# Sixteen pairs of gate tiles of a two-block model, each computed as seven half-width products instead of two full-width tiles

## The reference, cut to what matters

```python
h = rmsnorm_2(x, pre_norm_g[l])
proj = h @ w_in[l]
(u, v, z_a, c_q, c_kv, k_rope, z_b, x_c, z_c,
 g_a, g_b, g_c) = jnp.split(proj, cuts, axis=-1)
y_a = gmlp_spatial(u, v, ...) * jax.nn.silu(z_a)
y_b = mla_attention(c_q, c_kv, k_rope, ...) * jax.nn.silu(z_b)
y_c = rg_lru(x_c, ...) * jax.nn.silu(z_c)
merged = (jax.nn.sigmoid(g_a) * (y_a @ w_proj_a[l])
          + jax.nn.sigmoid(g_b) * (y_b @ w_proj_b[l])
          + jax.nn.sigmoid(g_c) * (y_c @ w_proj_c[l]))
x = x + rmsnorm_2(merged @ w_out[l], post_norm_g[l])
```

## Time and profile before

| | |
|---|---|
| median of 3 runs | 3152.47 us (3151.99 to 3153.68) |
| profiled execution, first to last instruction (span) | 3150.8 us |
| its PE busy time | 3140.4 us, 100% of the span |
| DVE, ACT, POOL busy | 59%, 40%, 13% |
| granted TensorE clock, mean | 1.000 |
| DMA | 110 GB/s on average |

### The profile page before, as it was taken

One profiled execution on the slowest core, in us unless ns is written; L12 is line 12 of the kernel. 1 busy time (PEld: TensorE's weight loads), 2 busy tenths in 40 slices (PEclk: granted clock), 3 DMA queues, 4 the chain that ended last, 5 costly groups with the idle time before them and its releaser, 6 DMA issues.

```text
span 3150.8 us, 36896 instructions
## 1 busy us (share of the span) xinstructions
PE 3140.4 (100%) x14840; PEld 2628.4 (83%) x14840; DVE 1859.9 (59%) x2504; ACT 1258.6 (40%) x1889; POOL 394.9 (13%) x287
## 2 busy tenths in 40 slices
PE   9999999999999999999999999999999999999999
PEld 8888888888888888888888888888888888888887
DVE  6876456665687655665557642447656754344754
ACT  4323334434433334443445422226635442223742
POOL 1201112110020121112012000110011100011001
PEclk9999999999999999999999999999999999999999
DMA  4332323235442223222642232223332222323432
GB/s 170 116 101 94 101 94 108 100 123 191 149 121 96 97 89 113 96 98 97 204 144 88 78 102 92 89 94 118 124 132 73 82 94 96 98 87 96 138 99 102
DMA packets 105354, 345.42 MB, mean 110 GB/s; under 512 B 13824, under 2 KB 14080, under 8 KB 104416
## 3 DMA queue, kind: packets, MB, share of 16 engines
q1 hardware_dynamic: 101856, 328.47, 32.1%
q0 software_dynamic: 3184, 14.06, 1.3%
q10 hardware_dynamic: 144, 0.52, 0.1%
HBM read 324.65 MB, written 2.10 MB: 104 GB/s over the span
## 4 chain that ended last, share of the span: by engine, by line
PE 96%; DVE 3%; ACT 1%; DMA 0%; SPq 0%; issue 0%; POOL 0%; POOLq 0%
PE ps L520 94%; DVE r L1484 1%; PE ps L611 1%; DVE wl L1474 1%; PE ps L852 0%; DVE f L1489 0%; SPq L2261 0%; DVE f L1552 0%; DMA X<-x_in 0%; DMA f<-f 0%; DVE r L1900 0%; DVE f L1722 0%; ACT wh L982 0%; ACT f L1308 0%; DVE sm L1921 0%; PE ps L564 0%
## 5 line engine op out<-in xcount | busy, mean ns | idle before, releaser
L520 PE MATMUL ps<-h,wh 128*128 128x512 f32 (+1 forms) x5824 | 1695.3, 375 | 0.7 <-DVE wl L1474 0.3
L520 PEld LDWEIGHTS ps<-h,wh 128*128 128x128 f32 x5824 | 1063.4, 188 | 200.1 <-issue 3.4
L520 PE MATMUL ps<-h,wl 128*128 128x512 f32 (+1 forms) x2912 | 1091.2, 375 | 0.0
L1474 DVE TENSOR_TENSOR wl<-raw,wh 128x1024 fp32r<-128x1024 f32 (+1 forms) x583 | 739.1, 1280 | 294.9 <-ACT wh L982 293.7
L982 ACT CAST wh<-raw 128x1024 fp32r<-128x1024 f32 (+2 forms) x596 | 592.3, 1006 | 685.9 <-PE ps L520 684.7
L520 PEld LDWEIGHTS ps<-h,wl 128*128 128x128 f32 x2912 | 547.1, 188 | 98.9
L520 PE MATMUL ps<-r,wh 128*128 128x512 f32 x1536 | 473.4, 389 | 0.9 <-DVE r L1484 0.5
L520 PEld LDWEIGHTS ps<-r,wh 128*128 128x128 f32 x1536 | 288.1, 188 | 62.2 <-issue 2.1
L1074 ACT CAST r<-f 128x512 fp32r<-128x512 f32 x194 | 119.8, 621 | 517.1 <-DVE f L1820 149.0
L520 PE MATMUL ps<-r,wl 128*128 128x512 f32 x792 | 304.3, 389 | 0.0
L520 PE MATMUL ps<-wh,r 128*128 128x512 f32 x960 | 302.4, 390 | 0.3
(11 more groups left out here) (160 smaller groups left out, 2133.5 us busy)
## 6 DMA issues: line engine op xcount, KB each, us to landing
raw<-wst SPq DMA_DIRECT2D x544, 512.0 KB, 3.3
raw<-wst SPq DMA_DIRECT2D x48, 320.0 KB, 3.0
r<-r SPq DMA_DIRECT2D x64, 128.0 KB, 2.3
f<-gains POOLq DMA_DIRECT2D x6, 1024.0 KB, 5.2
raw<-wst SPq DMA_DIRECT2D x20, 256.0 KB, 3.0
f<-f SPq DMA_DIRECT2D x72, 64.0 KB, 2.0
f<-tab POOLq DMA_DIRECT2D x16, 256.0 KB, 4.4
X<-x_in SPq DMA_DIRECT2D x4, 512.0 KB, 8.2
```

What stands on the lines that cost most here:

```text
L520: return e.matmul(o, a, b, start=start, stop=stop, skip_group_check=True)
L1474: e.tensor_tensor(l[:, 0:WIDTH[c]], raw[:, c % NRAW, 0:WIDTH[c]], h[:, 0:WIDTH[c]].bitcast(F32), ALU.subtract).then_inc(*lo_cut.up(("lo", c)))
```

## The change

In each of the two layers of the second block eight pairs of neighbouring gate tiles, gateb (3,4), (5,6), gatea and gatec (2,3), (4,5), (6,7), are computed together. A pair is a product of a 2x2 arrangement (first and second four tiles of k, first and second gate tile of the weights) with a 2x2 arrangement of h (first and second four tiles of k, first and second half of the rows). It is written in seven products of blocks in place of eight (Strassen's scheme in Winograd's form), each of 4 x 3 = 12 matmuls of 256 columns: p1, n5, p2, u2, p3, u3, c21. Around them:

- *Weights.* Four sums of weight blocks of a pair (128x512 each) are made by POOL (`sums`). The seven blocks (three raw, four sums) are cut in pieces of 512 columns, as chunks *0 to *3.
- *h.* Four combinations of h's blocks (`mixed`, 128x1024 each) are made once per layer by POOL (`mix`: ten steps of two pieces of 128x2x256) behind the first head's scores; ACT casts and DVE takes the low part of one of them at each of the heads 3 to 6. They lie where X was: X is saved to DRAM at the layer's start (`save_rows`) and loaded back at its end (`rows_back`).
- *Combining.* ACT copies p1, n5, u2 and u3 out of PSUM (`kept`, line 1329, 128x256). DVE makes c11, c12, c22 (lines 1984 to 1993). The sigmoids take 128x256, 128x512 and 128x256 elements. TensorE waits for the copy of p1 before u2, of n5 before p3, of u2 before u3 and of u3 before c21; the two output products of the pair are placed between p3, u3 and c21 (in halves) and behind c21.
- *Order.* The four layer_norm steps move from beside prb_0 to prb_3 to: behind pair 1, behind pair 2, and ahead of the gating of tiles 5 and 7. Three chunks more are cut ahead at the recurrence's last step. The sigmoids of gateb_1, gateb_2, gatec_0 and gatec_1 move.

The core of the diff:

```diff
+            def two_tiles(L, name, between):
+
+                c = NAME[f"{name}*0"]
+                first, second, third = (take((name, i)) for i in "abc")
+                product(first, name, 0, 0, quarter(0, 0), True).then_inc(*group_done.up(("done", (name, "p1"))))
+                for m in "1643":
+                    w.wait_ge(*at("mixed_lo", L, m))
+                product(second, name, 0, 1, combined("1"), True).then_inc(*group_done.up(("done", (name, "n5")), ("closed", c)))
+                product(third, name, 1, 0, quarter(0, 1), True, True).then_inc(*group_done.up(("done", (name, "p2"))))
+                w.wait_ge(*at("copied", name, "p1"))
+                product(first, name, 1, 1, combined("6")).then_inc(*group_done.up(("done", (name, "u2")), ("closed", c + 1)))
+                w.wait_ge(*at("copied", name, "n5"))
+                product(second, name, 2, 0, combined("4"), False, True).then_inc(*group_done.up(("done", (name, "p3"))))
+                between(0)
+                w.wait_ge(*at("copied", name, "u2"))
+                product(first, name, 2, 1, combined("3")).then_inc(*group_done.up(("done", (name, "u3")), ("closed", c + 2)))
+                between(1)
+                w.wait_ge(*at("copied", name, "u3"))
+                product(first, name, 3, 0, quarter(1, 1), False, True).then_inc(
+                    *group_done.up(("done", (name, "c21")), ("closed", c + 3)))
+                between(2)
...
+            def two_gates(L, b, j, first, second, then):
...
+                w.wait_ge(*at(*gate_free(L, b, j)))
+                kept(g0[:, lo], "a", "p1")
+                kept(g0[:, up], "b", "n5")
+                first()
+                w.wait_ge(*at(*gate_free(L, b, j + 1)))
+                kept(g1[:, lo], "a", "u2")
+                w.wait_ge(*at("c11", name))
+                e.activation(g0[:, lo], g0[:, lo], ACT.Sigmoid).then_inc(*act_tile.up(("gate11", name)))
+                second()
+                kept(g1[:, up], "a", "u3")
+                then(0)
...
+            def two_gates(L, b, j, n, first, second, then):
...
+                e.tensor_tensor(g0[:, lo], g0[:, lo], bank((name, "c"))[:, lo], ALU.add).then_inc(
+                    *dve_tile.up(("c11", name), ("free", (name, "c"))))
+                first()
...
+                e.tensor_tensor(g1[:, lo], bank((name, "b"))[:, lo], g1[:, lo], ALU.subtract).then_inc(
+                    *dve_tile.up(("c12", name), ("free", (name, "b"))))
+                second()
+                w.wait_ge(*at("copied", name, "u3"))
+                e.tensor_tensor(g1[:, up], g0[:, up], g1[:, up], ALU.subtract).then_inc(*dve_tile.up(("c22", name)))
+                then(0)
+                gated(L, b, 2 * n)
+                then(1)
+                gated(L, b, 2 * n + 1)
...
+                    if b == "b":
+                        small_step("layer_norm", L, n)
...
+                for q, (a, b) in enumerate(((one[:, 0:S], two[:, 0:S]), (t[0], two[:, S:2 * S]), (two[:, 0:S], two[:, S:2 * S]),
+                                            (t[1], one[:, S:2 * S]))):
+                    w.wait_ge(*at(*sums_free(name, q)))
+                    if q in (1, 3):
+                        w.wait_ge(*at("sums", name, q // 2))
+                    e.tensor_tensor(t[q], a, b, ALU.add).then_inc(*pool_tile.up(("sums", name, q)))
```

More of the change, by code:

```diff
@@ L122, in proj, with gate, product @@
         def proj(nm, w, nk, b):
[L123 to L128, removed]
+            def gate(j):
+                one(f"gate{nm}_", D2["gate"] + 1024 * b, j)
+            def product(j):
                 if nk == 8:
@@ L696, in gate_proj @@
                         tile(f"{L}/gate{g}_{j + n}", xs)
                     key = ("pr", L, b, j)
[L698 to L701, removed]
+                    name = f"{L}/pr{p}_{j - j % 2}"
+                    if j % 2 == 0:
+                        slot(name)
+                    h, l = weights(name)
+                    o = take(key)
+                    for k in range(4):
+                        w.wait_ge(*at(*ready, k))
@@ new lines, in gate_proj, with product @@
+                    last = group(o, h, l, [(j % 2 * 4 + k) * P for k in range(4)], ys)
+                    closes = (("closed", NAME[name]),) if j % 2 else ()
+                    last.then_inc(*group_done.up(("done", key), *closes))
+            def product(o, name, q, second, xs, start=False, stop=False):
+                c = NAME[f"{name}*{q}"]
+                h, l = split_at(c)
+                w.wait_ge(*at("lo", c, second))
+                for k, (xh, xl) in enumerate(xs):
+                    col = second * S + k * P
+                    last = three(o[:, halves(0)], h[:, col:col + P], l[:, col:col + P], xh, xl, start and k == 0, stop and k == 3)
+                return last
@@ L705, in gate_proj @@
                             w.wait_ge(*at(*ready, k))
[L706 to L720, removed]
-                            last.then_inc(*group_done.up(("closed", NAME[name]), *ends))
+                        last = group(o, h, l, [(k - k0) * P for k in part], [ys[k] for k in part], part[0] == 0,
+                                     part[-1] == len(ys) - 1)
@@ new lines, in some @@
+                        ends = (("done", key),) if part[-1] == len(ys) - 1 else ()
+                        ends += (("closed", NAME[name]),) if part[-1] == k0 + n - 1 else ()
+                        if ends:
+                            last.then_inc(*group_done.up(*ends))
+                whole = range(len(ys))
+                cut = len(ys) // 2
+                if b == "b":
+                    banks.let_go(f"{L}/gateb_1")
+                    banks.let_go(f"{L}/gateb_2")
+                else:
+                    for j in range(2):
+                        tile(f"{L}/gate{b}_{j}", xs)
```

451 lines of the change are left out of this document (351 added, 100 removed).

## The result

The changed kernel takes 3162.04 us (median of 7, 3161.48 to 3164.82) against 3152.47 us before (median of 7, 3151.30 to 3154.28): a ratio of 1.0032 with a 95% interval of 1.0021 to 1.0043. It is slower by about 9.6 us, where 3149 us was forecast (3.5 us less, too little to measure) and 3139 to 3160 us given as the range. The profiled execution took 3161.48 us, 1.3 us above its span of 3160.2 us. (Before, the profiled execution took 3151.99 us, 1.2 us above its span; the other 0.5 of the 1.7 us that the forecast added is scatter between executions.)

What follows compares the result with a forecast made beforehand. The prediction took TensorE, busy 3140.4 of 3150.8 us, as the bound. 18.0 us saved against 14.6 us of waits (7.3 per layer) gave 3147.4, plus 1.7 for the median: 3149 us, range 3139 to 3160.

Steps and rivals of the forecast that it cites:

- saving of the seven products: TensorE, 16 pairs: 768 full-width matmuls (174.1 us) replaced by 1344 half-width ones (156.1 us), 18.0 us saved, between 16.0 and 21.8.
- wait at the c start: First pair of c: u2 waits for ACT's copy of p1 behind the recurrence's cast; 4.0 us per layer, between 3.0 and 5.5.
- b, second pair: The normalization on DVE delays the chunk of prb_2; TensorE waits 2.0 us per layer, between 1.0 and 3.3.
- a, first pair: POOL's sums are just in time if undisturbed, mutual holds with DVE delay them; 1.0 us per layer, between 0.3 and 2.3.
- attention and before gatec_0: Attention: POOL's mix, DVE's low parts and ACT's casts added; 0.3 us wait per layer, between 0 and 1. Nothing before gatec_0.
- the rival of a shut-out in many pairs: POOL's sums hold DVE beyond 1.2 us to spare; 1.2 us wait in each of 10 pairs, 12 us, 3161; chance 0.10.
- plus what POOL's sums take from the scan chain on DVE (0 to 2.1 ...): Start of c: POOL's sums lengthen DVE's scan chain by 0 to 2.1 us, raising the wait from 3.4 to 4.0 per layer.
- the clock as a rival of 6 in 100: Waits at the c starts drop TensorE to 1.2 GHz for 5.6 us of work each; 11 us added, 3160; chance 0.06.
- I go two thirds of the way to it: 116.2 ns: Half-width matmuls in the pairs priced at 116.2 ns, between the trace's paces of 113.3 and 117.6; 156.1 us in all.
- POOL gets 40 pieces of mix: Attention: POOL gets 40 pieces of mix at 1.29 us each, about 52 us, where it had 2 of 110 us.
- The worst end of the sum: Smallest saving, 16.0 us, with the largest waits in both layers: +8.2 us, 3161.
- the weight-load rival: TensorE: half-width matmuls with changing weights held at 125 ns by the weight load; saving only 6.1 us, 3161; chance 0.04.

Runs made afterwards that it cites:

- e7: The changed kernel with the reorderings of e1 (start of c) and e6 (first normalization) together; 3146.67 us, ratio 0.9984 to the kernel before.
- e1: The changed kernel with p1/n5 copies and weight pieces ahead of the recurrence's end on ACT and DVE at the c start; 3150.24 us, ratio 0.9996.
- e2: The changed kernel with only the copies of p1 and n5 of gatec_2 moved ahead of the recurrence's last square root; 3159.62 us.
- e3: The changed kernel without POOL's four weight sums of gatec_2 in both layers, raw halves split in their place; 3154.86 us.
- e6: The changed kernel with DVE's first normalization in b moved from behind the first pair to behind prb_2's chunk; 3159.25 us.
- e5: The changed kernel with wl padded and shifted again as in the kernel before, DMA scratch 512 bytes in place of 1024; 3162.33 us.
- e4: The kernel before with only the low weights wl put in flat slots, without shift or padding, as in the changed kernel; 3153.32 us.
- e10: As e9, with POOL's four sums of gatec_2 held back until DVE has made gatec_1's low part; 3141.12 us, ratio 0.9965.
- e8: As e7, with wl in padded, shifted slots as in e5; 3145.98 us, ratio 0.9979.
- e9: As e8, with ACT also cutting *3 and prc_0 before the recurrence's last square root and its table load; 3143.02 us, ratio 0.9972.

## Why the prediction was wrong

The forecast was 3149 us with a net of -3.4 us; measured are +9.4 in the span. By its own terms (forecast, measured, both for two layers):

| term | forecast | measured |
|---|---|---|
| saving of the seven products | -18.0 | -14.5 |
| wait at the c start | +8.0 | +10.7 |
| clock behind it | 0 | +3.7 |
| b, second pair | +4.0 | +3.7 |
| a, first pair | +2.0 | +1.8 |
| attention and before gatec_0 | +0.6 | +2.6 |
| pace of the half-width products elsewhere | 0 | +1.8 |
| rest | 0 | -0.4 |
| sum | -3.4 | +9.4 |

The largest misses of the table are the clock (3.7 us), the saving (3.5), the wait at c (2.7) and the attention with the wait before gatec_0 (2.0); no one term explains the 12.8 us between forecast and result. The saving is from e7, where b has no wait: (70.72 - 68.91) / 2 pairs = 0.905 us a pair, times 16. The clock's share is what the c stretch lost beyond its wait: 102.92 - (98.30 - 3 x 0.905) - 5.33 = 2.0 us, and 1.7 in the second layer. Attention in the second layer is 1.1 us longer than before, in the first 0.2; that POOL's mix does this is likely, but no run left it out. The 0.9 us before gatec_0 come twice, and some 0.5 us of small waits that the second layer had before are gone.

**Right.** What bounds the kernel, and the three places where it would wait, each with its mechanism: the copy of p1 behind the recurrence's end (e1, e2; without the sums its wait is 3.3 us, e3, where the prediction had 3.4 before it added them), the normalization in front of prb_2's low part (1.64 us of wait for 2.0; e6), the sums at the start of a, where TensorE pauses 0.3, 0.1 and 0.2 us between products. At a, DVE's pieces of 512 columns take 1.8 us each beside the sums and 0.68 behind them:

```profile
2029.79 1.79 DVE L1722 TENSOR_TENSOR wl<-f,wh 128x512 fp32r<-128x512 f32 x1
2031.51 1.77 DVE L1722 TENSOR_TENSOR wl<-raw,wh 128x512 fp32r<-128x512 f32 x1
2033.20 0.68 DVE L1722 TENSOR_TENSOR wl<-f,wh 128x512 fp32r<-128x512 f32 x1
```

This place is read from the trace alone; no run changed it. TensorE doesn't wait for X at a boundary, as foreseen. In the other pairs there is no wait: the rival of a shut-out in many pairs, with its 1.2 us to spare, did not come.

**Wrong: "plus what POOL's sums take from the scan chain on DVE (0 to 2.1 ...)".** This is the step whose mechanism failed, and by e3 it cost most: about 6.2 us in the two layers (waits, the 0.9 us before gatec_0 and part of the clock) where the sum has 0.6 a layer. I counted one or two operations of the last scan. The sums run earlier, from 2233.55 to 2241.55, and meet four operations on DVE that all stand before the last scan, because DVE works without a break there: 3.7 us (e3). The wait came out at 5.3 us, within its 3.0 to 5.5, but only because TensorE itself started the pair 0.9 us late by the same holds, which the sum did not have at all.

**Wrong: the clock as a rival of 6 in 100 beside the sum.** With a forecast wait of 4 us twice and no wait over 1.1 us in the trace to judge by, the fall belonged into the sum's bounds: the sum put it at nothing. Waits of 5.3, 4.4 and 3.3 us were each followed by the level of 1.2 GHz, waits of 1.6 us were not. It cost 1.7 to 2.0 us each in the changed kernel (1.5 to 2.8 by the same working in e2, e3, e5 and e6), less than the rival's 5.6: the low level was granted for about 4 us, of which half is lost, and the rival had it for 5.6 us of work, which would take 11.

**Wrong: "I go two thirds of the way to it: 116.2 ns".** All pairs run at 117.6 ns, the pace of the row that stood in the same position; with it the sum would have given 16.0. Another 1.5 us go at the changes of width, which have about 0.02 us each on the first matmuls (three of 512 columns from 2262.17 take 0.70 us for 0.68). And the change took the fast pace from products that it does not touch, by the new place of wl (e4): an edit that the prediction does not mention, as no instruction changes by it.

**Slips that changed little.** "POOL gets 40 pieces of mix" counts both layers as one: a layer has 20, which took 29.7 us, not 52. 768 x 215.8 ns less 1344 x 109.2 ns are 19.0 us, not 18.9. The worst end of the sum is 3161 us, yet the range was cut at 3160. The 125 ns of the weight-load rival stand in no row; the pairs ran at 117.6.

## What to carry to other kernels

Where a new product waits for a copy on an engine whose program is written in order, put the copies and the weight pieces ahead of the serial chain of the old stage, and look at once for what is late next: here the copy, the weight pieces, a table load and POOL's sums stood one behind the other, and only all of them together gave back 15 us in two places (from the changed kernel to e10). Work for an engine that is over 80% idle is not free if it shuts out a busy one just where that one carries a serial chain. Judge a wait of several us on TensorE by its length and by what the clock does behind it. A product that is faster by count of matmuls has to be priced at the pace of the rows that stand in its own position.

## What the runs showed of the hardware

Half-width fp32r matmuls with changing weights have two paces, 113.3 and about 118 ns. Moving wl alone to other addresses removed the fast one everywhere (16 of 48 runs to none, e4; none either in any other trace with wl so placed); with wl moved back 17 runs were fast in e5, and 11, 10 and 10 in e8, e9 and e10. Within a pair it came only behind a pause of 0.1 to 0.3 us inside or ahead of a run, and it ended at the next 512-column matmuls or, in e8 and e9, at another such pause. So the place of the weights is needed and does not suffice. Which property of them matters was not tried. In one execution the clock fell in the attention behind two waits of 0.54 and 1.00 us; in others, with waits alike, it did not.
